# Folding a second norm into the up projection of a two-block kernel: raw X1 times the norm's weights goes in, the shift as two further columns, the tokens' factor behind it

## The reference, cut to what matters

```python
mod = silu(c) @ w_mod + b_mod                    # six vectors of width 2048
sh1, sc1, g1, sh2, sc2, g2 = split(mod, 6)
...
x = x + g1 * (merged @ w_o)                      # "merge" gives merged, "out" is w_o
h = rms_norm(x, norm2_g) * (1 + sc2) + sh2       # rms_norm: x * rsqrt(mean(x*x) + eps) * g
a, b = split(h @ w_up, 2)                        # "up": 2 x 5632 columns
a = dwconv_grid(a, dw, db)                       # 3 x 3, per channel, on a 4 x 64 grid
x = x + g2 * ((silu(a) * b) @ w_down)            # "down"
```

## Time and profile before

| | |
|---|---|
| three executions | 2338.14, 2338.18, 2333.81 us |
| profiled execution, its span | 2333.71 us, 2331.9 us |
| PE busy | 2265.9 us, 97% |
| DVE busy | 1647.5 us, 71% |
| ACT busy | 983.5 us, 42% |
| DMA | 475.62 MB, mean 204 GB/s |
| granted TensorE clock | mean 0.992 of full speed |

### The profile page before, as it was taken

How to read it: one execution, slowest core, us unless ns; L and a number is a source line. 1 busy time by engine, 2 the same in 40 slices (tenths; PEclk the granted TensorE clock), 3 DMA queues, 4 the chain that set the end, 5 groups by cost and what they waited for, 6 DMA issues and landing times.

```text
span 2331.9 us, 48670 instructions
## 1 busy us (share of the span) xinstructions
PE 2265.9 (97%) x18378; PEld 2178.9 (93%) x18378; DVE 1647.5 (71%) x2555; ACT 983.5 (42%) x1369; POOL 8.4 (0%) x18
## 2 busy tenths in 40 slices
PE   4899999999999999989999999999999999999999
PEld 3688888999999999989999999999999999999999
DVE  4465655899986666988878888875556666667764
ACT  3323222454543343444444444444445444444442
POOL 0000000000000000000000000000000000000000
PEclk7999999999999999999999999999999999999999
DMA  9965465443456677984555554555556444434443
GB/s 404 389 253 216 182 236 194 166 142 127 142 190 261 235 254 270 339 342 165 192 184 189 188 180 180 181 206 179 196 185 208 162 160 144 161 144 162 144 177 129
DMA packets 69511, 475.62 MB, mean 204 GB/s; under 512 B 7728, under 2 KB 9776, under 8 KB 18384
## 3 DMA queue, kind: packets, MB, share of 16 engines
q1 hardware_dynamic: 68688, 467.59, 55.2%
q0 software_dynamic: 768, 7.26, 0.9%
HBM read 469.58 MB, written 5.24 MB: 204 GB/s over the span
## 4 chain that ended last, share of the span: by engine, by line
PE 82%; DVE 9%; issue 2%; ACT 1%; DVEq 1%; ACTq 0%
PE acc L766 79%; PE aux L766 3%; DVE lo L1128 3%; DVE ar L1347 1%; DVE qla L1340 1%; DVE sc L1319 1%; DVE tt L1345 0%; DVE qlb L1340 0%; DVE raw L1138 0%; PE aux L1023 0%; DVE yab L1144 0%; ACT hi L461 0%; DVE yab L1145 0%; DVE hxu L1145 0%; ACT n L637 0%
## 5 line engine op out<-in xcount | busy, mean ns | idle before, releaser
L1128 DVE TENSOR_TENSOR lo<-raw,hi 128x1024 fp32r<-128x1024 f32 (+1 forms) x716 | 811.5, 1167 | 191.8 <-ACT hi L461 188.0
L461 ACT ACTIVATE hi<-raw 128x1024 fp32r<-128x1024 f32 (+1 forms) x716 | 695.4, 1011 | 311.4 <-PE acc L766 250.7
L766 PE MATMUL acc<-hx,hi 128*128 128x256 f32 (+1 forms) x3072 | 661.8, 312 | 7.1 <-DVE lo L1128 2.6
L766 PEld LDWEIGHTS acc<-hx,hi 128*128 128x128 f32 x3072 | 495.6, 188 | 43.9 <-issue 5.1
L766 PE MATMUL acc<-hxu,hi 128*128 128x256 f32 x2816 | 502.4, 282 | 8.0 <-DVE hxu L1145 7.8
L766 PE MATMUL acc<-hx,lo 128*128 128x256 f32 (+1 forms) x1536 | 474.0, 309 | 0.0
L766 PEld LDWEIGHTS acc<-hxu,hi 128*128 128x128 f32 x2816 | 432.2, 189 | 9.1 <-issue 7.8
L766 PE MATMUL acc<-hxu,lo 128*128 128x256 f32 x1408 | 394.4, 280 | 0.0
L766 PE MATMUL acc<-u,hi 128*128 128x272 f32 (+1 forms) x2048 | 382.3, 287 | 0.0
L766 PEld LDWEIGHTS acc<-u,hi 128*128 128x128 f32 x2048 | 317.3, 188 | 4.4 <-issue 2.5
L766 PEld LDWEIGHTS acc<-hx,lo 128*128 128x128 f32 x1536 | 288.9, 188 | 17.6
(11 more groups left out here) (292 smaller groups left out, 2285.7 us busy)
## 6 DMA issues: line engine op xcount, KB each, us to landing
raw<-wts SPq DMA_DIRECT2D x390, 1024.0 KB, 4.8
raw<-wdown SPq DMA_DIRECT2D x64, 704.0 KB, 4.2
xc<-xct SPq DMA_DIRECT2D x1, 4096.0 KB, 12.5
rawx<-wts SPq DMA_DIRECT2D x2, 1024.0 KB, 25.1
x<-xct SPq DMA_DIRECT2D x1, 2048.0 KB, 9.7
park<-x POOLq DMA_DIRECT2D x1, 2048.0 KB, 10.2
xf<-park POOLq DMA_DIRECT2D x1, 2048.0 KB, 9.3
outt<-outs SPq DMA_DIRECT2D x16, 128.0 KB, 3.8
```

The source lines that it names most:

```text
L461: A.activation(HI[:, slot, a:b, 0:P], RAW[:, p % 4, a:b, :], ACT.Copy).then_inc(hi_half, 1)
L766: return pe.matmul(*a, **k)
L1128: V.tensor_tensor(LO[:, slot, a:b, 0:P], RAW[:, p % 4, a:b, :], HI[:, slot, a:b, 0:P].bitcast(F32), ALU.subtract).then_inc(lo_half, 1)
```

## The change

Four things are changed, in the words of the code:

1. The 16 modulation units that went with "out" (column vectors of g2) go with "merge", whose columns now have two modulation units each. The order of the units in memory follows.
2. Behind "merge", DVE finishes `MODV` and `AM2`, writes the high and low part of the shift sh2 into two further token columns (256 and 257, both the same) of `HXU`, and clears `AT`. In "out", ACT writes the high part of `X1` times `AM2` into `HXU` (new L630), and DVE the low part (new L1476), per feature block. The stage with `N2` between "out" and "up" is gone. The two matmuls of the sum of squares stand in the middle of the first "up" product.
3. "up" multiplies 258 columns instead of 256. Column 256 of a product is its shift term.
4. In "up", DVE copies that column of the a product to a small tile, multiplies the product by `RS2` into `U1`, and ACT then makes `AT` from `U1` plus the column, and `CV` from `AT` (waiting for it). For the b product DVE copies the column, multiplies by `RS2` into `V1`, and the product with the SiLU becomes an instruction that adds the column too.

```diff
-    ("merge", 4, "sssmsssmsssmsssm"),
-    ("out", 4, "smsmsmsm"),
+    ("merge", 4, "sssmm" * 4),
+    ("out", 4, "ssss"),
...
# ACT, "out"
+                    A.activation(HXU[:, 0, j, 0:T], X1[:, j, :], ACT.Identity, scale=AM2[:, j:j + 1]).then_inc(z_high, 1)
# ACT, between
-            for g in range(4):
-                act.wait_ge(n2_ready, g + 1)
-                for k in range(4):
-                    j = 4 * g + k
-                    ins = A.activation(N2[:, 4 * (g % 2) + k, :], N2[:, 4 * (g % 2) + k, :], ACT.Identity, bias=MODV[:, 48 + j, 0:1],
-                                       scale=AM2[:, j:j + 1])
-                ins.then_inc(h2_aff, 1)
# ACT, "up"
-                    A.activation(AT[:, 1:5, 1:GRID + 1], ACC[:, 2 * jj, 0:T].rearrange("p (r c) -> p r c", c=GRID), ACT.Copy)
-                    A.activation(CV[:], ACC[:, 2 * jj, 0:T], ACT.Identity, scale=vcd("dw", 4 * FF + j),
-                                 bias=vcd("db", j)).then_inc(a_copied, 1)
+                    act.wait_ge(u1_ready, 2 * j + 2)
+                    ch.link(A.activation(AT[:, 1:5, 1:GRID + 1], U1[:].rearrange("p (r c) -> p r c", c=GRID), ACT.Identity,
+                                         bias=SMALL[:, 28:29]))
+                    A.activation(CV[:].rearrange("p (r c) -> p r c", c=GRID), AT[:, 1:5, 1:GRID + 1], ACT.Identity,
+                                 scale=vcd("dw", 4 * FF + j), bias=vcd("db", j)).then_inc(a_copied, 1)
# PE, "up": the first product is peeled, sums() are the two matmuls of the squares
+                    prod("up", i, p, lambda k: HXU[:, 0, k, 0:T + 2], lambda k: HXU[:, 1, k, 0:T + 2], lambda k: ACC[:, p, 0:T + 2],
+                         inputs=hx2_ready if first else None, needs={0: 12, 12: 13, 13: 14, 14: 15, 15: 16} if first else None,
+                         between=sums if first else None)
# DVE, "merge"
                     mod_unit("merge", i, p + 3, 4 * KD + j, CROWB)
-                    lo("merge", i, p + 4)
+                    mod_unit("merge", i, p + 4, 5 * KD + j, CROWB)
+                    lo("merge", i, p + 5)
# DVE, "out"
-                    mod_unit("out", i, 2 * jj + 1, 5 * KD + j, CROWB)
+                    dve.wait_ge(z_high, j + 1)
+                    V.scalar_tensor_tensor(HXU[:, 1, bass.ds(j, 1), 0:T].rearrange("p a t -> p (a t)"), x1, AM2[:, bass.ds(j, 1)],
+                                           HXU[:, 0, bass.ds(j, 1), 0:T].rearrange("p a t -> p (a t)").bitcast(F32),
+                                           ALU.mult, ALU.subtract).then_inc(hx2_ready, 1)
# DVE, "up"
+                    done("up", i, 2 * jj)
+                    dve.wait_ge(rs2_done, 1)
+                    V.tensor_copy(SMALL[:, 28:29], ACC[:, 2 * jj, T:T + 1]).then_inc(u1_ready, 1)
+                    V.tensor_tensor(U1[:], ACC[:, 2 * jj, 0:T], RS2[:], ALU.mult).then_inc(u1_ready, 1)
...
+                    done("up", i, 2 * jj + 1)
+                    mark(V.tensor_copy(SMALL[:, 29:30], ACC[:, 2 * jj + 1, T:T + 1]))
+                    link(V.tensor_tensor(V1[:], ACC[:, 2 * jj + 1, 0:T], RS2[:], ALU.mult))
                     dve.wait_ge(cv_sig, 1 + j + 1)
-                    V.tensor_tensor(CV2[:], ACC[:, 2 * jj + 1, 0:T], S1[:], ALU.mult).then_inc(bank_free, 1)
+                    V.scalar_tensor_tensor(CV2[:], V1[:], SMALL[:, 29:30], S1[:], ALU.add, ALU.mult).then_inc(bank_free, 1)
+                    dve.wait_ge(x1_out, 16)
```

More of the change, by code:

```diff
@@ L398, in _ @@
             with sp.Fori(0, ITERS["out"]) as i:
-                for p in range(8):
+                for p in range(4):
                     load("out", i, p)
@@ L621, in _ @@
             tables(LOGEXP)
-            with act.Fori(0, ITERS["out"]) as i:
+            act.wait_ge(am2_ready, 1)
+            for i in range(ITERS["out"]):
                 for jj in range(4):
-                    hi("out", i, 2 * jj + 2)
-                    act.wait_ge(bank_free, prod_index("out", i, 2 * jj) + 1)
+                    hi("out", i, jj + 1)
+                    act.wait_ge(bank_free, prod_index("out", i, jj) + 1)
+                    j = 4 * i + jj
+                    A.activation(HXU[:, 0, j, 0:T], X1[:, j, :], ACT.Identity, scale=AM2[:, j:j + 1]).then_inc(z_high, 1)
                     act.wait_ge(s2_added, 1 + 4 * i + jj)
-                    A.activation(SQ2[:, jj % 2, :], X1[:, bass.ds(4 * i + jj, 1), :].rearrange("p a t -> p (a t)"),
-                                 ACT.Square).then_inc(sq2_done, 1)
+                    A.activation(SQ2[:, jj % 2, :], X1[:, j, :], ACT.Square).then_inc(sq2_done, 1)
             act.wait_ge(ss2_mm, 1 + 1)
@@ L656, in _ @@
                     A.activation(S1[:], CV[:], ACT.Silu).then_inc(cv_sig, 1)
+            ch.leave(ITERS["up"], "a_up")
             tables(LOGEXP)
@@ L975, in _, with sums, up_columns @@
                 for jj in range(4):
-                    prod("out", i, 2 * jj, lambda k: MRG[:, 0, k, 0:T], lambda k: MRG[:, 1, k, 0:T], lambda k: ACC[:, jj, 0:T],
+                    prod("out", i, jj, lambda k: MRG[:, 0, k, 0:T], lambda k: MRG[:, 1, k, 0:T], lambda k: ACC[:, jj, 0:T],
                          inputs=mrg_ready if jj == 0 else None, each=4)
[L978 to L983, removed]
-                for p in range(4):
-                    prod("up", i, p, lambda k: HXU[:, 0, k, 0:T], lambda k: HXU[:, 1, k, 0:T], lambda k: ACC[:, p, 0:T],
-                         inputs=hx2_ready if p == 0 else None)
+            def sums():
+                pe.wait_ge(s2_added, 1 + KD)
+                mm(AUX[:, 0, 0:T], ONESR[:], S2[:], start=True, stop=False)
+                pe.wait_ge(sq2_done, 1 + KD)
+                mm(AUX[:, 0, 0:T], ONESR[:], SQ2[:, 1, :], start=False, stop=True).then_inc(ss2_mm, 1)
+            def up_columns(i, peeled=False):
+                for p in range(4):
+                    first = peeled and p == 0
+                    prod("up", i, p, lambda k: HXU[:, 0, k, 0:T + 2], lambda k: HXU[:, 1, k, 0:T + 2], lambda k: ACC[:, p, 0:T + 2],
+                         inputs=hx2_ready if first else None, needs={0: 12, 12: 13, 13: 14, 14: 15, 15: 16} if first else None,
+                         between=sums if first else None)
+            up_columns(0, True)
+            with pe.Fori(1, ITERS["up"]) as i:
+                up_columns(i)
             with pe.Fori(0, ITERS["down"]) as i:
@@ L1442, in _ @@
             GSIG += 2 * KD
+            link(V.tensor_tensor(MODV[:, 4 * KD:6 * KD, 0], MODV[:, 4 * KD:6 * KD, 0], vc("bmod", 4 * KD, 2 * KD), ALU.add))
+            V.scalar_tensor_tensor(AM2[:], MODV[:, 64:80, 0], 1.0, vc("norm2", 0, KD), ALU.add, ALU.mult).then_inc(am2_ready, 1)
+            dve.wait_ge(am2_ready, 1)
+            sh2 = MODV[:, 48:64, 0:1].broadcast_to([P, KD, 2])
+            link(V.tensor_copy(HXU[:, 0, :, T:T + 2], sh2))
+            link(V.tensor_tensor(HXU[:, 1, :, T:T + 2], sh2, HXU[:, 0, :, T:T + 2].bitcast(F32), ALU.subtract))
+            ch.straight()
+            V.memset(AT[:], 0.0).then_inc(cv_ready, 1)
             dve.wait_ge(in_x1, 16)
@@ L1793 @@
     for j in range(KD):
-        order += [wi[64 + j], wi[80 + j], pba[j], wmt[4 * KD + j]]
+        order += [wi[64 + j], wi[80 + j], pba[j], wmt[4 * KD + j], wmt[5 * KD + j]]
     for j in range(KD):
-        order += [wo[j], wmt[5 * KD + j]]
+        order += [wo[j]]
     for j in range(FF):
```

41 lines of the change are left out of this document (13 added, 28 removed).

## The result

The changed kernel took 2362.42 us, the median of four executions from 2359.82 to 2363.66; the kernel before 2337.39 us in the same comparison. The ratio is 1.0112, with a 95% interval from 1.0100 to 1.0124: slower by 25 us between the medians, 26 us by the ratio. The profiled execution took 2363.11 us, its span is 2361.1.

A forecast was written before the change was run, and what follows sets the result against it. PE was taken to bound the kernel before, DVE "up" after. +2.2 - 8.4 + 30.1 + 0.7 = +24.6 us on the profiled 2333.71 gave 2358.3, stated as 2359 because the median lay higher; range 2344 to 2375.

The forecast's parts named there:

- PE bounds before, DVE after: In "up", DVE's cycle of 12.06 us per pair against PE's 11.44 makes DVE the bound: +30.1 us over 43 pairs.
- The gap behind "out": Between "out" and "up", DVE reaches its first tap at 1045.6 instead of 1053.99: -8.4 us.
- First column of "merge": In "merge", the added modulation unit stands ahead of a `lo` that is already late: +2.2 us.
- My rival on the clock: In "up", short PE waits lower the granted clock, 2.8 us more per pair, total over 2400; chance 0.03.
- Steady columns of "merge", and "out": The added unit in "merge" falls where DVE waits for ACT; PE sets the pace in "out": 0 for both.
- Only about 0.7 us per pair is slack against PE.: In "up", of DVE's 1.79 us wait per pair, 1.05 is ACT's path, which DVE must spend whenever it comes.
- the first rival: In "up", PE keeps the pace, DVE's cycle at most 11.44 us: -4.8 us, 2329; chance 0.08.
- 258 columns: In "up", two more columns per matmul cost at most in proportion: 0.04 us per product, 3.4 us over 43 pairs.
- rival 1: In "up", PE keeps the pace with added DVE instructions hidden in the 1.79 us of waiting: 2329 us; chance 0.08.
- The pointer operand: In "up", ACT's first instruction, with a pointer for its bias, costs about 0.50 us instead of 0.39.

The follow-up runs named there:

- the idle products: The kernel before with idle DVE products of 0.34, 1.02 or 2.28 us at the head of each "up" pair: ratios 1.0002, 0.9999 and 1.0075.
- the half `lo`: The changed kernel with the second half of the b unit's `lo` moved behind `U1` in "up": 2342.36 us, ratio 1.0022.
- merge_only: The kernel before with only the modulation units of "out" moved to "merge": 2339.04 us, ratio 1.0010.

## Why the prediction was right

The forecast was 2359 us, measured 2362.42. Point by point:

- *PE bounds before, DVE after.* Right. The chain went from 9% to 20% DVE, and the cycle is 12.09 us where the sum gave 12.06. The added parts came out as follows: the copies 0.06 to 0.07 each instead of 0.10, ACT's first 0.51 for 0.50, the handover between ACT's two 0.18 instead of 0.04, the second 0.60 for 0.56, its end to the tap 0.15 for 0.21. The path at the head is 1.96 instead of 1.87, the copy and `V1` ahead of the SiLU product 0.61 instead of 0.64, and all the rest 9.46 instead of 9.49. That the cycle is met to 0.03 is in part luck, since the errors cancel; the prediction's own bounds for it were 11.6 to 12.5. DVE's wait is 1.48 us where about 1.3 was named, and PE stands 12.09 - 11.57 = 0.5 us per pair where 0.6 was.
- *The gap behind "out".* -8.6 for -8.4; PE's wait for the second `lo` 1.86 us, where 1.7 was expected:

```profile
1048.16 0.48 PE L766 MATMUL acc<-hxu,hi 128*128 128x258 f32 x2 [1.86 <-DVE lo L1137]
```

- *First column of "merge".* +2.2 as forecast, and about +1.5 by the granted clock behind it, which the sum left out. My rival on the clock had put it in "up", where the clock stayed at 1.00 with about 0.5 us of waiting per pair.
- *Steady columns of "merge", and "out".* Nothing in the steady columns, as forecast: 17.05 us per column with one unit or two. "Out" gained 0.6 us at its head, which the sum had at 0, since its window began just before the wait ended.
- *"Only about 0.7 us per pair is slack against PE."* Wrong, as the idle products showed: it was 1.79. The step counted ACT's 1.05 us as time that DVE must spend whenever it comes. That holds once `U1` stands ahead of ACT, not before. The sum didn't rest on it, since the cycle was added up from DVE's work and the new path. But a reader who took that sentence to another edit would be off by 1 us per pair, and the first rival was argued against with it.
- *258 columns.* Taken "at most in proportion", 0.04 us per product. Measured 0.10. In the changed kernel it doesn't count, since DVE sets the pace (read from the chain; no run has the changed kernel with 256 columns). It decides what any repair can reach, and rival 1's time of 2329 was too low for that reason.
- *The size of the total.* 25 us between the medians and 26 by the ratio, against a sum of 24.6. Between the traces it is 29.2, of which 2.6 lie ahead of the change; the 2.0 that then remain over the sum are 1.3 in the pairs and 0.9 in "merge" and "out", less 0.2.
- *The range.* Cycles of 11.65 to 12.5 us put into the prediction's own sum give 2341 to 2378 us; the range of 2344 to 2375 was drawn tighter than that. The measured time lies well inside both.
- *The pointer operand.* The prediction sets "free affine" against 93 ns per pointer operand, both from the Trainium skill, ScalarE: Activation LUTs. The 93 ns stand where it says; "free affine" stands in the section "Step-by-step: what each stage is for". The first instruction took 0.51 us instead of 0.39, but it also reads another tile (`U1`, not `ACC`), so the 0.12 aren't the pointer's alone.

## What to carry to other kernels

A wait of an engine is room only as long as what it waits for doesn't start from that engine's own work. An elementwise step that is put between PE and another engine's step turns a path that ran beside into one that runs in series. Its price is then the work it adds and the part of the path that nothing covers, less the room that was there: here 1.04 + 1.48 - 1.79 = 0.73 us per pair, and not the 0.4 us of the step itself. Fill the wait that it makes with the next independent piece, as the half `lo` did, before judging the idea; and count what the further columns of a matmul cost on the chip before spreading two of them over 4224 matmuls.

## What the runs showed of the hardware

- A matmul of 258 or 260 columns came every 120.5 ns, of 256 every 118.3, of 264 every 121.7: two columns cost 2.2 ns, eight 3.4.
- After a wait of PE of 2.60 us the granted clock of the next 4 us was 0.68 in one kernel (after) and 0.59 in another (merge_only, where the first matmuls came every 0.21 us instead of 0.12). After one of 0.38 us at the same place, in the kernel before, it was not lowered (the row below), and in "up", with waits of 0.3 us in every pair, it stayed at 1.00.

```profile
686.50:690.00 3.50, 3.33 (x28) 3.36 (x29) 3.40 (x8) 0.89 (x1) 0.00 (x0) 1.00 1.03 339
```

- Two ACT instructions, of which the second waits for the first, started 0.69 us apart, the first taking 0.51; two independent ones started 0.28 apart, the first taking 0.39.
